# The opening of a two-branch layer kernel: input tiles in three groups with conditioning halves between them, square sums from rows, and a first round with its own order

## What is computed

```python
ada = (silu(c) @ w_ada + b_ada).reshape(B, 9, 1024)     # c: 9 conditioning vectors (1 prompt, 8 samples)
xn  = x * rsqrt(mean(x * x) + 1e-6) * g_ffn1 * (1 + ada[:, 1]) + ada[:, 0]
x   = x + 0.5 * ada[:, 2] * ((silu(xn @ w_gate) * (xn @ w_up)) @ w_down)      # hidden width 2816
# then a mixer (RG-LRU and spatial gating), a second SwiGLU of the same form, a final norm
```

## Time and profile before

| | us |
|---|---|
| median of 3 runs | 2484.96 (2484.96 to 2490.06) |
| the profiled execution | 2487.25 |
| its span | 2485.5 |
| first product of round 0 starts | 84.60 |
| round 1 starts | 139.24 |
| TensorE busy | 2405.7 (97% of the span) |
| VectorE busy | 1674.5 (67%) |
| ScalarE busy | 1053.8 (42%) |
| GpSimd busy | 147.5 (6%) |
| moved by DMA | 381.03 MB, 153 GB/s on average |

### The profile page before, as it was taken

One profiled execution on the slowest core, in us unless ns is written; L12 is line 12 of the kernel. 1 busy time (PEld: TensorE's weight loads), 2 busy tenths in 40 slices (PEclk: granted clock), 3 DMA queues, 4 the chain that ended last, 5 costly groups with the idle time before them and its releaser, 6 DMA issues.

```text
span 2485.5 us, 31914 instructions
## 1 busy us (share of the span) xinstructions
PE 2405.7 (97%) x11469; PEld 2029.7 (82%) x11469; DVE 1674.5 (67%) x2660; ACT 1053.8 (42%) x1825; POOL 147.5 (6%) x186
## 2 busy tenths in 40 slices
PE   7899999999899999999999999999999999989997
PEld 3577777777788877999999999997777788878886
DVE  4977767766666785656666665569677667656666
ACT  3454545444333353433443334245444444433334
POOL 3000000000000000000111110000000000000000
PEclk9899999999999999999999999999999999999998
DMA  9254554555876433312221213414545543497642
GB/s 358 72 170 153 181 175 149 165 188 195 321 266 229 136 127 105 130 54 63 63 63 55 62 38 116 159 56 134 170 145 168 174 139 121 166 355 267 228 136 79
DMA packets 245520, 381.03 MB, mean 153 GB/s; under 512 B 16657, under 2 KB 158153, under 8 KB 243990
## 3 DMA queue, kind: packets, MB, share of 16 engines
q1 hardware_dynamic: 232702, 345.15, 40.1%
q0 software_dynamic: 10240, 33.56, 4.8%
q10 hardware_dynamic: 2456, 0.75, 0.1%
HBM read 262.93 MB, written 116.47 MB: 153 GB/s over the span
## 4 chain that ended last, share of the span: by engine, by line
PE 81%; DVE 9%; DMA 4%; issue 3%; ACT 2%; SPq 1%; DVEq 0%; ACTq 0%
PE bank L514 23%; PE bank L515 23%; PE bank L516 23%; PE bank L2877 2%; PE bank L2880 2%; PE bank L2879 2%; DMA wraw<-in_w_ffn_down 2%; DVE u_lo L606 2%; DMA h_dram<-stage_lo 1%; PE bank L2895 1%; PE bank L2897 1%; DVE wraw L633 1%; DVE x L2185 1%; PE bank L2788 1%; DMA w_ada_sb<-in_w_ada 1%
## 5 line engine op out<-in xcount | busy, mean ns | idle before, releaser
L606 DVE TENSOR_TENSOR u_lo<-wraw,u_hi 128x512 fp32r<-128x512 f32 (+2 forms) x532 | 317.1, 617 | 277.8 <-ACT u_hi L600 274.8
L514 PE MATMUL bank<-ops,u_hi 128*128 128x512 f32 x1232 | 487.4, 396 | 3.9 <-issue 2.0
L515 PE MATMUL bank<-ops,u_hi 128*128 128x512 f32 x1232 | 484.7, 393 | 0.0
L516 PE MATMUL bank<-ops,u_lo 128*128 128x512 f32 x1232 | 483.3, 392 | 0.0
L600 ACT ACTIVATE u_hi<-wraw 128x512 fp32r<-128x512 f32 (+2 forms) x532 | 287.1, 567 | 249.5 <-PE bank L516 152.9
L514 PE MATMUL bank<-xn_hi,w_hi 128*128 128x384 f32 x1104 | 370.7, 336 | 5.2 <-ACT ww L1640 2.0
L515 PE MATMUL bank<-xn_lo,w_hi 128*128 128x384 f32 x1104 | 369.5, 335 | 0.0
L516 PE MATMUL bank<-xn_hi,w_lo 128*128 128x384 f32 x1104 | 369.4, 335 | 0.0
L514 PEld LDWEIGHTS bank<-ops,u_hi 128*128 128x128 f32 x1232 | 233.8, 190 | 67.1 <-issue 5.9
L516 PEld LDWEIGHTS bank<-ops,u_lo 128*128 128x128 f32 x1232 | 233.7, 190 | 50.4
L515 PEld LDWEIGHTS bank<-ops,u_hi 128*128 128x128 f32 x1232 | 233.8, 190 | 49.0
(11 more groups left out here) (325 smaller groups left out, 4243.3 us busy)
## 6 DMA issues: line engine op xcount, KB each, us to landing
h_dram<-stage_hi SPq DMA_DIRECT2D x154, 256.0 KB, 2.5
h_dram<-stage_lo SPq DMA_DIRECT2D x154, 256.0 KB, 2.8
ada_raw<-in_w_ada POOLq DMA_DIRECT2D x96, 256.0 KB, 3.2
raw<-in_w_in SPq DMA_DIRECT2D x48, 512.0 KB, 4.7
wraw<-in_w_ffn_gate SPq DMA_DIRECT2D x44, 512.0 KB, 4.0
wraw<-in_w_ffn_up SPq DMA_DIRECT2D x44, 512.0 KB, 4.8
wraw<-in_w_ffn_down SPq DMA_DIRECT2D x48, 384.0 KB, 5.3
x<-x_dram SPq DMA_DIRECT2D x6, 2304.0 KB, 11.9
```

Of the source, the lines that this page charges most:

```text
L514: nc.tensor.matmul(out, hi, mov_hi, start=first, stop=False, skip_group_check=True)
L515: nc.tensor.matmul(out, hi, mov_lo, start=False, stop=False, skip_group_check=True)
L516: return nc.tensor.matmul(out, lo, mov_hi, start=False, stop=last, skip_group_check=True)
L606: nc.vector.tensor_tensor(unit(u_lo, f, g, u, n), unit_source(u, n), unit(u_hi, f, g, u, n).bitcast(F32), ALU.subtract).then_inc(u_lo_read ...
```

## The change

- The input tiles come in three groups with conditioning halves between them, and the halves in another order: first feature half of scale and shift, second feature half of both, then the gate's. The stores of `x` are four instead of two, each of one feature half and one token half, and the first goes out ahead of the third group of tiles, when eight blocks are in place.
- The sums of squares are taken from the tiles as they lie in rows, before they are turned: ScalarE's square with an accumulated output gives one value per token in one partition (`row_squares`), root and reciprocal are made on 4, 4 and 1 columns, and TensorE spreads them over partitions (`spread`), from where ScalarE copies them (`factor_copy`). The sixteen squares, GpSimd's fourteen additions, the sums with ones and the 512-column reciprocals go.
- The first product needs only half 0 and 1. Halves 2 to 5, the third group of tiles and the samples' operand (now in two halves, in `xs_made`) are worked into round 0, which gets its own order (`opening_round`): A11, samples, S1, A12, samples, S2, S3, A22, S4.
- In round 1 the third piece of `w_ada` is made at the end of round 0's list, ahead of three stage copies, and the fourth ahead of the seventh.
- What `first_half` and `prompt` of TensorE are given as a last argument is called after their second step.

```diff
-FIRST_HALVES = [(v, half) for v in (SCALE1, SHIFT1, GATE1) for half in range(2)]
+FIRST_HALVES = [(SCALE1, 0), (SHIFT1, 0), (SCALE1, 1), (SHIFT1, 1), (GATE1, 0), (GATE1, 1)]
+FIRST_BANKS = (7, 6, 7, 2, 7, 7)
...
@@ SyncE @@
-            for t in range(3):
-                tile_rows(sp, t)
+            tile_rows(sp, 0)
...
-            sp.wait_ge(x_loaded[1], 16)
             ada_half(0)
+            tile_rows(sp, 1)
             ada_half(1)
-            first_weights(0)
+            weights(0, 0, 0, 0)
+            weights(0, 0, 1, 0)
+            sp.wait_ge(x_in, 8)
+            spill(slice(0, KH), x_spilled, slice(0, PH))
+            tile_rows(sp, 2)
             ada_half(2)
+            weights(0, 0, 0, 1)
+            weights(0, 0, 1, 1)
             ada_half(3)
             sp.wait_ge(x_in, 2 * NT)
-            spill(slice(0, KH), x_spilled)
-            spill(slice(KH, KT), x_spilled_late)
+            spill(slice(0, KH), x_spilled_late, slice(PH, TOK))
+            sp.wait_ge(x_spilled, 16)
+            spill(slice(KH, KT), x_spilled, slice(0, PH))
+            sp.wait_ge(sumsq_mm, 9)
             ada_half(4)
+            sp.wait_ge(x_spilled_late, 16)
+            spill(slice(KH, KT), x_spilled_late, slice(PH, TOK))
             sp.wait_ge(rg_loaded, 64)
...
@@ GpSimd @@
             pool.wait_ge(x_turned, 12)
+            pool.wait_ge(sumsq_mm, 6)
             nc.gpsimd.memset(rg_sb[:, :, :, :], 0.0).then_inc(rg_zeroed, 1)
-            add_squares(0)
             load_pieces(0)
...
@@ ScalarE @@
+            def row_squares(lo, hi):
+                for t in range(lo, hi):
+                    act.wait_ge(x_loaded[t // 3], 32 if t >= 6 else 16)
+                    if t > 1:
+                        act.wait_ge(sumsq_mm, t - 1)
+                    nc.scalar.activation(spent[:, t % 2, :], xrow[:, t, :], ACT.Square, accum_out=nrst[:, t:t + 1])\
+                      .then_inc(sumsq_mm, 1)
...
             def op_hi(f, o, tiles=slice(0, KH)):
-                if f == 0 and o == O_T3:
+                if f == 0 and o in (O_B11, O_B21):
+                    act.wait_ge(ada_ready, 2 if o == O_B11 else 4)
+                elif f == 0 and o == O_T1:
+                    act.wait_ge(ada_mm, 2)
+                elif f == 0 and o == O_T3:
                     act.wait_ge(ada_mm, 5)
...
                 def after_first_joins():
...
                     unit_hi(act, f, 1, 7)
+                    pieces(1, 3)
                     stage(0, 3, h_sum, 1, g11)
...
+                def opening_round():
+                    op_hi(f, O_B11)
+                    row_squares(6, NT)
+                    root(0, 1)
+                    root(0, 2)
+                    begin(0)
+                    unit_hi(act, f, 0, 4)
+                    unit_hi(act, f, 0, 5)
+                    begin_up(0)
+                    factor_copy(0, 1)
+                    factor_copy(0, 2)
...
+                    op_hi(f, O_T1)
+                    first_rows(2)
+                    samples_hi(f, 0)
+                    unit_hi(act, f, 0, 6)
+                    unit_hi(act, f, 0, 7)
+                    first_rows(3)
...
                 def round_(g):
...
                     pieces(g, 2)
-                    pieces(g, 3)
+                    if g > 1:
+                        pieces(g, 3)
+                    else:
+                        pieces(g, 4)
+                        unit_hi(act, f, g, 8)
+                        unit_hi(act, f, g, 9)
                     stage(g - 1, 6, h_sum, 4, g21)
...
-            squares(0, 0, KT)
...
+            row_squares(0, 3)
             act.wait_ge(sp_step, 1)
             nc.scalar.activation(spw[:, 1, :], spw[:, 0, :], ACT.Exp, scale=-1.0).then_inc(sp_exp, 1)
-            squares(0, KT, 2 * KT)
-            squares_of_samples(0)
+            row_squares(3, 6)
+            root(0, 0)
             first_rows(0)
+            factor_copy(0, 0)
+            first_units(0)
             first_rows(1)
...
@@ VectorE @@
             def op_scale(f, kk, c):
+                dve.wait_ge(samples_act, FACTORS_MADE[i, c])
+                if f == 0:
+                    dve.wait_ge(mod_step, 1 if kk < KH else 2)
+                    dve.wait_ge(*((x_spilled, x_spilled_late)[c], 16 if kk < KH else 32))
...
+                def opening_round():
+                    x_turned_in(2)
+                    reciprocal(0, 1)
+                    reciprocal(0, 2)
+                    weight_sum(dve, f, 0, 1)
+                    weight_sum(dve, f, 0, 2)
+                    unit_lo(dve, f, 0, 4)
+                    unit_lo(dve, f, 0, 5)
+                    for k in range(KH):
+                        op_scale(f, k, 1)
+                    for k in range(KH):
+                        op_sum_(f, O_T1, k)
+                    first_samples(0)
+                    first_samples_shifted(0)
+                    op_lo(f, O_T1)
+                    first_samples_lo(0)
+                    for i in range(3, 7):
+                        weight_sum(dve, f, 0, i)
+                    first_half(2)
...
+                    op_lo(f, O_T2)
...
+                    first_half(4)
+                    op_lo(f, O_T3)
...
+                    op_lo(f, O_T4)
+                    first_half(5)
+                    op_lo(f, O_B22)
+                    end_of_first()
...
-            dve.wait_ge(x_in, 2 * NT)
             dve.wait_ge(sp_step, steps[0])
+            x_turned_in(1)
+            dve.wait_ge(x_in, 12)
+            reciprocal(0, 0)
             first_half(0)
+            dve.wait_ge(ada_ready, 1)
+            scale_gain(SCALE1, 0, KH)
+            for u in range(4):
+                unit_lo(dve, 0, 0, u)
+            for k in range(KH):
+                op_scale(0, k, 0)
             first_half(1)
...
+            op_lo(0, O_B11)
             ffn(0)
...
@@ TensorE @@
+            pe.wait_ge(rows_copied, 1)
             first_half(0)
+            x_turn(1)
             first_turn(0)
+            def first_factors():
+                pe.wait_ge(x_in, 12)
+                spread(0, 0)
+            first_half(1, first_factors)
             first_turn(1)
...
+                def opening_round():
+                    prompt(0, A11[0], O_B11, X[0], True, False, True)
+                    x_turn(2)
+                    prompt(0, A11[1], O_B11, X[1], True, False)
+                    pe.wait_ge(x_in, 2 * NT)
+                    spread(0, 1)
+                    spread(0, 2)
+                    first_half(2)
+                    first_half(3, lambda: first_turn(2))
+                    pe.wait_ge(xs_lo_ready, 1)
+                    samples_in(0, 0)
+                    first_turn(3)
+                    prompt(0, S1[0], O_T1, Z[0], True, False, True)
...
+                    prompt(0, A12[0], O_B21, W[0], True, True, True)
...
+                    samples_in(0, 1)
+                    first_half(4)
+                    pe.wait_ge(snapped, snaps(f, 0, 1))
+                    prompt(0, S2[0], O_T2, X[0], False, False, True, lambda: first_turn(4))
...
+                    first_half(5)
+                    pe.wait_ge(snapped, snaps(f, 0, 3))
+                    prompt(0, S3[0], O_T3, X[0], False, False, True, lambda: first_turn(5))
...
```

More of the change, by code:

```diff
@@ L114 @@
                                (1, 4, True), (1, 6, True)]
-SQUARES = ([(c, k, False) for c in range(2) for k in range(KT)],
+SQUARES = ([],
            FFN1_SQUARES,
@@ L152, in added, with squares_done, summed_squares, sample_steps @@
 def added(i, pos):
-    return sum(is_added(j, q) for j in range(i) for q in range(NSQ)) + sum(is_added(i, q) for q in range(pos))
+    return sum(is_added(j, q) for j in range(1, i) for q in range(NSQ)) + sum(is_added(i, q) for q in range(pos))
+def squares_done(i, pos):
+    return NSQ * (i - 1) + pos + 1
+def summed_squares(i, c):
+    return (4, 8, 9)[c] if i == 0 else 9 + 3 * (i - 1) + RANK[i][c]
+def sample_steps(i):
+    return 3 * i + 3 if i > 0 else 0
 def ring_use(i, pos):
@@ L1170, in first_units @@
             def first_units(f):
-                for u in EARLY:
+                for u in (EARLY if f == 1 else range(4)):
                     unit_hi(act, f, 0, u)
@@ L2102, in first_round @@
                 def first_round():
-                    if f == 0:
-                        for k in range(KH):
-                            op_scale(f, k + KH, 0)
-                        op_lo(f, O_B21)
                     sample_operand(f)
```

432 lines of the change are left out of this document (218 added, 214 removed).

## The result

The changed kernel takes 2470.34 us (median of four runs, 2468.48 to 2471.52), the kernel before 2484.96: ratio 0.9936, 95% interval 0.9924 to 0.9949. That is 14.6 us less where 24.0 had been forecast (2484.96 against 2461). The time lies inside the stated range of 2451 to 2473, but outside the forecast's own range of 2456 to 2467. Later runs of the kernel before have medians of 2483.04 (16 runs), 2484.30 (7) and 2482.16 us (13), so the change is worth 12 to 15 us. The profiled execution took 2471.01 us, against 2487.25.

A forecast was written before the change was run, and what follows sets the result against it. The opening was taken as bound by the DMA queue, with VectorE busy and TensorE's lead small in round 0. Gains of 17.2 (round 0) and 6.5 (round 1), 23.7 us, gave 2463.6, adjusted to the runs' median 2461; range 2451 to 2473.

The forecast's parts named there:

- the forecast's own range: Whole kernel: 2456 to 2467 us around the forecast of 2461, given a chance of 0.55.
- the late pieces: Rival in round 1: only the pieces of w_ada stay late, 2468 us; chance 0.21 shared with the late queue.
- the late queue: Rival in round 0: second store lands near 62 us, one more low-clock stretch, 2472 us; chance 0.21 shared with late pieces.
- First product: Opening: first product at 36.9 us against 84.6, needing only halves 0 and 1 and two groups of tiles.
- Polynomial: VectorE's chain for the gate's constant: steps 0.17 us instead of 1.18 without GpSimd's additions, chain 4.4 instead of 11.4 us.
- its other bound: Polynomial steps stay at 1.18 us: chain ends at 28 to 30 us and the sum is 2.5 us worse.
- Second store and row: Round 0: store releases VectorE near 54 us, conditioning row 2 turned at 61.0, round ends at 122.0, gain 17.2 us.
- slower: Rival: gaps among round 0's products keep TensorE's clock low; gain gone at a third of 77 us, 2500 at half; chance 0.04.
- its 2.4 us: Round 0, charged behind the wait inside half 3: low clock, the excess of a half taking 9.45 against 7.04 us.
- Round 1: Waits for w_ada pieces with their low clock make the round 7.5 us too long; earlier pieces gain 6.5 us (bounds 0 and 7.5).
- no wait over 1 us at L2895's successor: Sign: with round 1 starting at 122 us, TensorE no longer waits over 1 us there.
- From round 2 on nothing is bound to the clock on the wall: Later rounds: the change touches about the first 190 us, and what is won there should arrive at the end.

The follow-up runs named there:

- the row ahead: Changed kernel with ScalarE's copies of the second row's product (first_rows(2)) put ahead of its split of the third operand: 2469.85 us.
- the store ahead: Changed kernel with SyncE's second store of the inputs put ahead of the loads of conditioning half 3 instead of behind them: 2471.63 us.
- the repeat: The changed kernel measured once more with no edit: 2469.76 us, ratio 0.9945.
- the all-early kernel: Changed kernel with the last pieces and units of every round ahead of the seventh stage, and round 1's ScalarE units 10 and 11 too: 2462.48 us.

## Why the prediction was right, and where it was not

The opening came out as forecast, by the mechanism of the forecast. The sum is 9.3 us too low, because round 1 was priced too high and nothing was charged for the later rounds. The time falls where two of the rivals stood, the late pieces (2468) and the late queue (2472), without being either: the second store released VectorE at 52.11 and not near 62, and round 1 did gain. That the time lies in the range owes something to the second network's gain, which the forecast didn't know of.

**First product: right.** 36.11 us, forecast 36.9. Half 0 began at 15.3 (16.2), its matmuls took 7.04 as priced, the tiles' copies 3.68 for six, 0.6 each. VectorE's timeline of the changed kernel has the polynomial's step, the copies behind it and the scaling behind the second store:

```profile
18.04 0.17 DVE L1867 TENSOR_SCALAR spw<-spw 128x8 f32<-128x8 f32 x1
...
23.04 3.68 DVE L1829 COPY x<-bank 128x512 f32<-128x512 f32 x6 [1.79 <-PE bank L2862]
...
52.11 2.74 DVE L1941 SCALAR_TENSOR_TENSOR x<-x,ada,acc 128x512 f32<-128x512 f32 x4 [4.55 <-DMA x_dram<-x]
```

**Polynomial: right, and its other bound holds as far as can be told.** All seven steps took 0.17 us. With GpSimd's additions put back they took 1.13 to the end of those additions. The rule of the Trainium skill, "SBUF — State Buffer", Who interferes with whom, that the forecast leaned on is borne out by that run: a blocked step of 1.13 us beside 0.17. For the other case the forecast had 7 us on VectorE's chain and 2.5 us in the sum. The run with additions has 7.1 us on the chain (12.1 against 5.0), and a median 2.4 to 3.0 us longer. Its round 0 ended 5.4 us late, but only 2.4 against the opening whose half 0 was as slow. The forecast was too low on the way: VectorE came 4 to 6 us late to the tiles and the first product 5 to 7, most of which the later waits absorbed.

**Second store and row: right within 2.6 us.** The store released VectorE at 52.11 (54) after a wait of 4.55 us (some 7), the row was turned at 58.45 (61.0), and TensorE stood still for 3.18 us, less than the 5 to 8 expected. Round 0's end gained 18.6 us (17.2). The runs add what the sum had left unsaid: of two ways to shorten this stretch neither showed a gain in the time by itself; with the row ahead the next wait took it back, with the store ahead half 3 came late.

**Low clock: there, in another place.** The stage from 36.1 to 120.6 us had a granted clock of 0.98, so the rival "slower" was never near. The forecast took its 2.4 us for a floor, after the rule of the Trainium skill, "TensorE: Matmul & The Clock Gate", What's actually happening, that the high clock has to be earned by activity. In this trace about 1.7 us of it shows (0.02 of 84.5 us), which is under the floor; in the same stretch the repeat had 0.96, about 3.4 us, which is over it. So the size depends on the execution. And it doesn't stand where the sum had it: behind the 3.18 us wait the last twelve matmuls of half 3 took 5.32 us, the pace of 7.04 for sixteen, while the first product's matmuls from 37.00 us on took 0.63 us each instead of 0.39. More scatter of this kind stands in the last section.

**Round 1: the failed step.** "So round 1 has 7.5 us too much" and "Gain **6.5 us**". The subtraction was wrong: from the milestone to the round's start lie 3.0 us, not 6.4, and the all-early kernel has a whole round 1, milestone to milestone, in 48.1 us against 53.0. The excess was 4.9. And "the third piece now comes before the stage copies, the fourth right after" counted both waits of the earlier trace rows as gone: only the first goes. The second belongs to a piece that stands behind the seventh stage, which the change left where it was. With it the sign "no wait over 1 us at L2895's successor" failed: 1.94 us at 144.96, and three more behind round 2. In six of the seven other runs that have this part, round 1 is 3.6 to 3.7 us shorter than before; the 1.9 of the first profile has a stretch of low clock in it (0.96 over the round), as has the 2.1 of the run with additions (0.97).

**The second network: overlooked.** "Everything outside the first 190 us is the same work in the same order" holds of the opening only. `round_` and `after_first_joins` serve both networks, so the second one's first round was changed as well and gained 3.6 us. Where no low clock falls into it, each of the two rounds gains 3.6 us, 7.2 together; the first profile has 1.9 and 3.6, the repeat 3.7 and 1.9. That 5.5 or 5.6 comes near the 6.5 forecast for one round is luck.

**"From round 2 on nothing is bound to the clock on the wall, and what is won there should arrive at the end": failed.** A settled round looks free, with TensorE busy in all of it, but ScalarE's stage waits in each for a store and TensorE's next piece stands behind it with little to spare. In round 4 the stage came 1.95 us later than before (17.06 us behind the milestone instead of 15.11) and TensorE waited 1.71, so the slack was 0.24. Three rounds of the first network lost 5.4 us so. The account against the 23.7 of the forecast is then 18.6 + 1.9 + 3.6 - 5.4 = 18.7; 0.9 us went between the networks, 2.0 came in round 5 of the second one, which has such a wait in both kernels (1.90 us before, 1.54 after) and took 50.6 us instead of 52.6 (granted clock 1.00 instead of 0.97), and 3.6 went in the tail: 16.2 us of the span.

## What to carry to other kernels

In a hand-written order, put what TensorE needs next ahead of anything that waits for a DMA to land, even where the wait looks hidden: the order of two entries in ScalarE's and VectorE's lists was worth 8 us here, beside 18.6 of the whole new opening. Before an opening is judged by one profile, see whether its clock was that of the profile it is compared with: here the same instructions differed by 1.5 us at the first product and by 3 at the end of round 0, more than either of the two edits of the opening. When helpers are shared, go through every caller before saying what stays the same. And price a "too much" between the same two milestones in both rounds.

## What was not expected of the hardware

- The same opening takes 117.4 to 120.6 us to the first milestone. The four at 117.4 to 117.9 have half 0 in 7.02 to 7.04 us; in the seven others, the edited openings among them, the granted clock fell there and it took 8.3 to 8.7. The window from 15 to 20 us in the changed kernel, then in the all-early one:

```profile
15.00:20.00 5.00, 5.00 (x18) 1.28 (x17) 3.76 (x22) 1.18 (x3) 0.00 (x0) 1.00 1.03 398
```

```profile
15.00:20.00 5.00, 4.90 (x9) 0.96 (x9) 4.07 (x24) 1.35 (x4) 0.00 (x0) 0.66 1.03 399
```

  There the half took 8.72 us instead of 7.04 and the first product came at 37.59 instead of 36.11, with nothing changed up to it.
- A late store landing stands in the same three rounds (4, 5 and 9 of the first network) in all eleven kernels with the new opening, moved by neither 5.4 us of delay nor up to 2336 more packets in the queue, and in none of the three with the old one. Another stands in round 5 of the second network in all fourteen. All but that of round 4 go with a 16 KB packet of the instruction queue in the same two microseconds; whether it is the cause no run tests.
- VectorE's small two-source steps are not safe beside GpSimd either: in the run with the additions one of 128x8 took 1.06 us (at 18.14) and the others 0.17.
